# Hosted modulation units spread over whole feed-forward stages, two wide groups in the delta stage, tables in eight pieces

## The reference, cut to what matters

```python
# first block, per layer (6 vectors of 1024)
mod = silu(c) @ ada_w[layer] + ada_b[layer]
# second block, per layer (9 vectors of 1024), for two conditions c and c_ctx
m = silu(cond) @ w_mod[l] + b_mod[l]
# every sublayer
h = rmsnorm(x) * (1 + scale) + shift
x = x + gate * sublayer(h)
# feed-forward, hidden width 2816
y = (silu(h @ w_gate) * (h @ w_up)) @ w_out
```

## Time and profile before

| what | value |
|---|---|
| median of 3 runs | 2902.71 us (2901.74 to 2904.06) |
| profiled execution | 2902.25 us |
| its span, first to last instruction | 2900.4 us |
| mean granted clock of PE | 0.946 |
| busy: PE, DVE, ACT | 2601.0, 1778.0, 1039.6 us |
| DMA | 407.56 MB, 141 GB/s in the mean |

### The profile page before, as it was taken

One profiled execution on the slowest core, in us unless ns is written; L12 is line 12 of the kernel. 1 busy time (PEld: TensorE's weight loads), 2 busy tenths in 40 slices (PEclk: granted clock), 3 DMA queues, 4 the chain that ended last, 5 costly groups with the idle time before them and its releaser, 6 DMA issues.

```text
span 2900.4 us, 37201 instructions
## 1 busy us (share of the span) xinstructions
PE 2601.0 (90%) x15014; PEld 2187.0 (75%) x15014; DVE 1778.0 (61%) x2929; ACT 1039.6 (36%) x1572; POOL 53.3 (2%) x56
## 2 busy tenths in 40 slices
PE   5789999787889889999797889999989999888998
PEld 4748998665789867878585567787868888766998
DVE  3546659643476688888836658787453333665655
ACT  4465445511244432222313432222242222434543
POOL 1000000021000000000000000000000000000000
PEclk8989999898899989999898999999999999899999
DMA  8675855434467646666422026575423332431563
GB/s 273 200 221 150 240 172 158 129 117 152 120 172 205 188 124 175 188 183 171 118 65 68 1 73 195 162 200 142 118 85 95 95 95 84 105 82 42 159 188 114
DMA packets 635648, 407.56 MB, mean 141 GB/s; under 512 B 27639, under 2 KB 596694, under 8 KB 634326
## 3 DMA queue, kind: packets, MB, share of 16 engines
q1 hardware_dynamic: 634800, 404.94, 48.6%
q10 hardware_dynamic: 678, 0.25, 0.0%
HBM read 404.09 MB, written 1.05 MB: 140 GB/s over the span
## 4 chain that ended last, share of the span: by engine, by line
PE 78%; DVE 12%; ACT 5%; DMA 2%; issue 2%; ACTq 0%; SPq 0%; POOL 0%; DVEq 0%
PE ps L1508 66%; DVE ada_acc L1759 3%; DVE tmp L1951 1%; PE ps L1519 1%; DVE h_lo L1943 1%; PE ps L1290 1%; PE ps L539 1%; DVE w_lo L1737 1%; PE ps L1267 1%; ACT w_hi L1628 1%; PE ps L801 1%; PE ps L809 1%; DMA wide_rows<-in_ada_w 1%; PE ps L811 1%; DMA raw<-in_attn_w_in 1%
## 5 line engine op out<-in xcount | busy, mean ns | idle before, releaser
L1508 PE MATMUL ps<-h_hi,w_hi 128*128 128x256 f32 (+1 forms) x3048 | 1021.5, 335 | 69.5 <-DVE h_lo L1943 59.4
L1628 ACT CAST w_hi<-raw 128x1024 fp32r<-128x1024 f32 (+3 forms) x557 | 554.8, 996 | 1387.3 <-PE ps L1508 1349.1
L1508 PE MATMUL ps<-h_hi,w_lo 128*128 128x256 f32 (+1 forms) x3048 | 1008.2, 331 | 0.0
L1508 PE MATMUL ps<-h_lo,w_hi 128*128 128x256 f32 (+1 forms) x3048 | 1007.9, 331 | 0.0
L1737 DVE TENSOR_TENSOR w_lo<-raw,w_hi 128x1024 fp32r<-128x1024 f32 (+3 forms) x557 | 644.9, 1158 | 363.5 <-ACT w_hi L1628 361.4
L1508 PEld LDWEIGHTS ps<-h_hi,w_hi 128*128 128x128 f32 x3048 | 589.5, 193 | 144.1 <-issue 69.5
L1508 PEld LDWEIGHTS ps<-h_lo,w_hi 128*128 128x128 f32 x3048 | 590.7, 194 | 50.5
L1508 PEld LDWEIGHTS ps<-h_hi,w_lo 128*128 128x128 f32 x3048 | 591.7, 194 | 47.6
L1508 PE MATMUL ps<-a_hi,w_hi 128*128 128x256 f32 (+1 forms) x1056 | 357.6, 339 | 0.1
L1508 PE MATMUL ps<-a_hi,w_lo 128*128 128x256 f32 (+1 forms) x1056 | 355.9, 337 | 0.0
L1508 PE MATMUL ps<-a_lo,w_hi 128*128 128x256 f32 (+1 forms) x1056 | 355.7, 337 | 0.0
(11 more groups left out here) (313 smaller groups left out, 1926.8 us busy)
## 6 DMA issues: line engine op xcount, KB each, us to landing
raw<-in_ffn_w_in SPq DMA_DIRECT2D x264, 512.0 KB, 4.6
ada_raw<-in_w_mod SPq DMA_DIRECT2D x128, 512.0 KB, 4.0
raw<-in_ffn_w_out SPq DMA_DIRECT2D x96, 512.0 KB, 4.6
wide_rows<-in_ada_w SPq DMA_DIRECT2D x64, 512.0 KB, 5.0
raw<-in_ffn_w_out SPq DMA_DIRECT2D x48, 384.0 KB, 3.4
raw<-in_gdn_w_in SPq DMA_DIRECT2D x33, 512.0 KB, 4.1
raw<-in_w_in SPq DMA_DIRECT2D x26, 512.0 KB, 3.8
raw<-in_attn_w_in SPq DMA_DIRECT2D x24, 512.0 KB, 7.0
```

The source lines that it names most:

```text
L1508: last = mm(ps[0:m, slot, 0:n], w[:, slot, k * P:k * P + m], v[:, s0 + k, 0:n], start=(k == 0 and w is w_hi and v is hi), stop=(k == lin.k ...
L1628: nc.scalar.copy(w_hi[:, slot, 0:n], raw[:, slot, 0:n]).then_inc(s_hi, 1)
```

## The change

The tiles of `HOSTS` span whole feed-forwards, across stage borders, and units are evenly spread over them: 2 first units in the projection as before; 8 first units over the 68 tiles of the first block's layer 0 feed-forward; none in layer 1's; 12 second units over feed-forward 1 and 10 over feed-forward 2 of the second block's layer 0; 8 over feed-forward 1 of its layer 1. There are two wide groups in the delta stage instead of three: group 2 with G = 0 and group 3 with G = 1, with products after levels 4, 5, 6 and after the first five state steps; turned and written at the end of each G. The tables come as eight DMAs, after tiles 4, 6, ... 18, and the three small DMAs after tile 6; angles are made at step 16, sines at step 20. A hosted pair is loaded at least three tiles after the one that it is used with.

```diff
-WIDES = (("first", 6, "attention", 6), ("first", 10, "attention", 7),
-         ("first", 16, "delta", 7), ("first", 20, "delta", 3), ("second", 0, "delta", 7))
+HOSTS = ((4, 2, ("attn_w_in", 0), ("attn_w_in", 0)), (14, 8, ("ffn_w_in", 0), ("ffn_w_out", 0)),
+         (30, 12, ("ffn1_w_in_2", 0), ("ffn1_w_out_2", 0)), (42, 10, ("ffn2_w_in_2", 0), ("ffn2_w_out_2", 0)),
+         (52, 8, ("ffn1_w_in_2", 1), ("ffn1_w_out_2", 1)))
+WIDES = ((6, "attention", 6), (10, "attention", 7), (22, "delta", 7), (26, "delta", 7))
+SECOND = 2 * 2 * MOD1
...
+def hosted_units(stages):
+    pairs, sums, order = {}, {}, {}
+    for unit0, count, first, last in HOSTS:
+        tiles = [s.g0 + j for s in stages if isinstance(s, Linear) and s.weight in (first, last) for j in range(s.n)]
+        for u in range(count):
+            a, b = (tiles[0] + (len(tiles) - 1) * (u + i) // count for i in range(2))
+            order[unit0 + u] = len(order)
+            for k in range(KD // 2):
+                g = a + k * (b - a) // (KD // 2)
+                pairs.setdefault(g, []).append((unit0 + u, k))
+            sums[g] = unit0 + u
+    return pairs, sums, order
...
@@ delta_tensor
-                    wide_products(pe, 2 + 2 * G, level)
-                wide_products(pe, 2 + 2 * G, 7)
+                    if level >= 4:
+                        wide_products(pe, 2 + G, level - 4)
                 for n, step in enumerate((turn, first_values, new_state, keys_by_state, second_values, outputs, output_sums)):
                     for s in range(2):
                         step(2 * G + s, s)
-                    if step is new_state:
-                        wide_turned(pe, 2 + 2 * G)
-                    if not G:
-                        wide_products(pe, 3, n)
-                if not G:
-                    wide_products(pe, 3, 7)
-                    wide_turned(pe, 3)
+                    if n < 5:
+                        wide_products(pe, 2 + G, 3 + n)
+                wide_turned(pe, 2 + G)
...
@@ SP
-            def load_tables():
-                sp.dma_start(consts[:, head:], dram["constants"][:, head:]).then_inc(s_rest, 16)
-                sp.dma_start(pos_i[:], dram["positions"].to_broadcast([P, T])).then_inc(s_rest, 16)
+            def load_table(n):
+                a, b = (head + (table.shape[1] - head) * (n + i) // 8 for i in range(2))
+                sp.dma_start(consts[:, a:b], dram["constants"][:, a:b]).then_inc(s_rest, 16)
+            def load_small():
+                sp.dma_start(pos_i[:], dram["positions"].to_broadcast([P, T])).then_inc(s_pos, 16)
...
-                if g == 8:
-                    load_tables()
-                for host, u, k in after_tile.get(g, ()):
-                    unit_pair(host, u, k)
+                if 4 <= g < 20 and g % 2 == 0:
+                    load_table(g // 2 - 2)
+                if g == 6:
+                    load_small()
+                for u, k in after_tile.get(g, ()):
+                    unit_pair(u, k)
...
+            in_order = [(g, pair) for g in sorted(pairs_at) for pair in pairs_at[g]]
+            for p, (g, pair) in enumerate(in_order):
+                earliest = in_order[p - 2][0] + 6 if p >= 2 else 0
+                after_tile.setdefault(max(earliest, g + 3), []).append(pair)
```

More of the change, by code:

```diff
@@ L133, with __init__ @@
 class Linear:
-    def __init__(self, kind, weight, kt, n, tokens, row0=0, offsets=None, stride=BODY * P, loads=None, ada=None, **more):
+    def __init__(self, kind, weight, kt, n, tokens, row0=0, offsets=None, stride=BODY * P, loads=None, **more):
         self.kind, self.weight, self.kt, self.n, self.tokens = kind, weight, kt, n, tokens
-        self.row0, self.offsets, self.stride, self.loads, self.ada = row0, offsets, stride, loads, ada
+        self.row0, self.offsets, self.stride, self.loads = row0, offsets, stride, loads
         self.more = more
@@ L151, in pieces @@
         return [(0, j // BODY * self.stride + self.offsets[j % BODY], P)]
[L153 to L168, removed]
     def columns(self, j):
@@ L236, in number @@
 def number(stages):
-    g = h_blocks = a_blocks = units = rows = norms = subs = silus = sqs = ssqs = 0
+    g = h_blocks = a_blocks = norms = subs = silus = sqs = ssqs = 0
     slot_dmas = [0] * RING
@@ L284, in number @@
         elif s[0] == "attention":
-            stages[i] = ("attention", h_blocks, units)
-            units += 4 * sum(w[2] == "attention" for w in WIDES)
+            stages[i] = ("attention", h_blocks)
             h_blocks += KD
         elif s[0] == "delta":
-            stages[i] = ("delta", h_blocks, units)
-            units += 4 * sum(w[2] == "delta" for w in WIDES)
+            stages[i] = ("delta", h_blocks)
             h_blocks += HEADS
@@ L498, in units_before @@
             i = next(n for n, s in enumerate(stages) if s is st)
[L499 to L506, removed]
+            earlier = [s[0] for s in stages[:i] if not isinstance(s, Linear)]
+            return FIRST_UNITS + sum(g < tiles_before(st) for g in sum_at) + 4 * sum(w[1] in earlier for w in WIDES)
         def blk(j, n=1):
             return proj[:, j * T:(j + n) * T]
-        def wide_before(n):
-            return WIDES[n][1] + (2 * 2 * MOD1 if WIDES[n][0] == "second" else 0)
         def wide_load(sp, n, k):
             i = KD * n + k
-            which, unit0, _, _ = WIDES[n]
-            name, per = ("ada_w", 2 * MOD1) if which == "first" else ("w_mod_2", 2 * MOD2)
             if i >= 2:
@@ L1067, in delta_vector @@
                         step(2 * G + s, s)
-                    if step is second_rhs:
-                        wide_columns(dve, 2 + 2 * G)
-                if not G:
-                    wide_columns(dve, 3)
+                wide_columns(dve, 2 + G)
         def delta_gpsimd(pool, st):
@@ L1510, in tile, with unit_sums @@
                 last.then_inc(s_tile, 1)
-            def unit_sums(lin, u):
-                dual = lin.ada[0] == "second"
-                pe.wait_ge(s_ada_use, KD * (lin.row_unit0 + u + 1))
-                pe.wait_ge(s_mod, lin.unit0 + u)
-                for c in range(2 if dual else 1):
+            def unit_sums(unit):
+                pe.wait_ge(s_ada_use, KD * (row_unit[unit] + 1))
+                pe.wait_ge(s_mod, unit)
+                for c in range(1 if unit < SECOND else 2):
                     for q in range(4):
@@ L1763, in ada_rows, with ada_sum @@
                     last.then_inc(s_ada_use, 1)
-            def ada_sum(lin, u):
-                which, first, _ = lin.ada
-                dve.wait_ge(s_ada_T, lin.row_unit0 + u + 1)
-                for c in range(2 if which == "second" else 1):
-                    last = V.tensor_reduce(mod_columns(which, c, first + u), ps[:, ADA_A + c, :].rearrange("p (q n) -> p q n", q=4), AX_X, ALU.add)
+            def ada_sum(unit):
+                dve.wait_ge(s_ada_T, row_unit[unit] + 1)
+                for c in range(1 if unit < SECOND else 2):
+                    dst = mod1[:, 4 * unit:4 * unit + 4] if unit < SECOND else mod2[:, c, 4 * (unit - SECOND):4 * (unit - SECOND) + 4]
+                    last = V.tensor_reduce(dst, ps[:, ADA_A + c, :].rearrange("p (q n) -> p q n", q=4), AX_X, ALU.add)
                 last.then_inc(s_mod, 1)
             def angles():
-                dve.wait_ge(s_rest, 64)
+                dve.wait_ge(s_pos, 16)
+                dve.wait_ge(s_rest, 160)
                 link(dve, V.tensor_copy(ang[:, 2, :], pos_i[:]), "dve")
@@ L1896, in _ @@
                             split(*nxt)
-                        for u in st.sums(j - 1):
-                            ada_sum(st, u)
-                        for u, k in st.pairs(j):
-                            ada_rows(st, u, k)
-                        if st.g0 + j == 10:
+                        if st.g0 + j - 1 in sum_at:
+                            ada_sum(sum_at[st.g0 + j - 1])
+                        for unit, k in pairs_at.get(st.g0 + j, ()):
+                            ada_rows(unit, k)
+                        if st.g0 + j == 16:
                             angles()
```

107 lines of the change are left out of this document (44 added, 63 removed).

## The result

The changed kernel takes 2865.26 us (median of 4 runs, 2864.54 to 2868.94) against 2903.39 us of the kernel before beside it: a ratio of 0.9871, 95% interval 0.9854 to 0.9888. The forecast was 2866.1 us. A second measurement on another occasion gave 2866.47 against 2903.14, ratio 0.9872 (0.9857 to 0.9886). The profiled execution took 2864.54 us with a span of 2862.7.

A forecast was written before the change was run, and what follows sets the result against it. PE was taken as full in feed-forwards, with waits for hosted sums on top. Feed-forwards 22.7, delta stage 9.4 and tables 5.5 us, less 1 for seams, saved 36.6, giving 2866.1 us; 8-in-10 range 2851 to 2885.

The forecast's parts named there:

- The yardsticks: Feed-forwards without hosted units, PE full: 368.3 us at 512 tokens, 190.3 at 256; anything beyond is the hosted units' price.
- part 1: Feed-forwards: evenly spread hosted units remove PE's waits where two pairs meet in one step; saves 22.7 us together.
- The price of a sum: PE's cost per hosted unit's sum: 0.9 us at 512 tokens, 1.7 at 256, 2.5 in a kt 6 stage.
- DMA in layer 0: First block's layer 0 feed-forward: 50.7 MB at 247 GB/s, hidden but only just; 1 us added, range 0 to 10.
- The delta stage: Part 2, fewer wide products in merge levels and five between state steps of each G: saves 9.4 us.
- State steps of G = 0: Delta stage, 35.2 us with nine wide products falls to 28.7 with five; saves 6.5 us, while G = 1 loses 0.7.
- outside DVE's work: Delta stage state steps: the part of five wide products' time that DVE's work does not cover, about 1.4 us.
- The projection: Part 3, tables in pieces: unit 4's last pair lands near 78.5, PE waits 4 to 5 us, not 9.3; saves 5.5.
- Crowding was not the cause: Rival for the feed-forwards: DVE stays late whatever the spacing, 20 us less gain, 2886 us; chance 0.12.
- More than counted: Rival: merge levels give 0.8 us each, state steps find their rows, some 256-token waits go; 2853 us, chance 0.12.
- Pieces cost like small DMAs: Rival for the projection: eight table pieces at 1.5 us each; part 3 loses 6 us, 2878 us; chance 0.04.
- the slower one: Rival: first block layer 0 becomes bound by DMA, under 210 GB/s; at 205 GB/s the kernel takes 2908 us; chance 0.02.

The follow-up runs named there:

- experiment 3: Changed kernel with 17 and 13 evenly spread hosted units in second block layer 0's feed-forwards 1 and 2, none in layer 1: 2878.17 us, ratio 0.9908.
- experiment 1: Changed kernel with PE transposing a hosted unit's sums one tile later: 2845.90 us, ratio 0.9794 of the kernel before.
- experiment 6: Changed kernel with each hosted pair of the first block's layer 0 feed-forward loaded twice, the second time into unread rows: 2873.41 us, ratio 0.9896.
- experiment 2: Changed kernel with wide products after every merge level and one after turn, instead of three in levels and five between state steps: 2854.38 us, ratio 0.9826.
- experiment 4: Changed kernel with the table in one DMA and the three small DMAs behind it, after tile 8: 2871.25 us, ratio 0.9883.
- experiment 5: Changed kernel with the table in sixteen pieces, one after each of tiles 4 to 19: 2865.66 us, ratio 0.9872.

## Why the prediction was right, step by step

**The yardsticks.** Everything in part 1 hung on two feed-forwards without hosted units, 368.3 and 190.3 us. They stayed: the last one takes 190.3 us after too, layer 1's feed-forward 1 is back at 368.3 in experiment 3, where it has no units, and with the hosts gone layer 1 of the first block takes 189.3, 1.0 less than its yardstick. I had held back 0.8 of its 8.3 us; nothing needed it.

**The price of a sum.** 0.9 us for a second unit at 512 tokens, 1.7 for a first one at 256, 2.5 in a kt 6 stage. After, 27 sums at 512 tokens outside kt 6 stages are all followed by the next tile without a wait; the three in kt 6 stages waited 2.35, 1.40 and 1.13 us; those at 256 tokens 1.02 to 1.03 in `swiglu` and 1.19 in `residual` stages, and 2.72 in the kt 6 one, for which I had only 2.5 with the transposes; with them it cost about 3.2. That mis-sized term is more than half of the 1.2 us by which the first block's layer 0 came out worse. The three long feed-forwards are within 0.7 us each. The causes given are shown by experiment 1 (the wait is where the sum stands) and, with the two limits found there, experiment 3 (crowding).

**DMA in layer 0.** Forecast hidden at 247 GB/s plus 1 us; it was 240 GB/s at a share of 0.81, and experiment 6 shows the room above. That the stage from 320.0 to 369.5 had hosted at this density was the right row to go by.

**The delta stage** was 2.4 us too good. Levels 1 to 3 lose 0.43 us each, not 0.45, right; but the first level with a product takes 7.26 us and not 6.60 (experiment 2), which I had not seen, 0.7 us in each G. From the start of the stage, or of G = 1, to level 6's product the two G gained 2.4 us together, forecast 3.6. State steps of G = 0 gained 6.2 of 6.5, and G = 1 lost 1.6 where 0.7 was forecast; these three make up the 2.4. Inside the state steps errors met that nearly cancel. The base after all subtractions was 23.8 us, from a stretch in which PE had its lower clock about a third of the time (that is what a mean of 0.82 between full and half clock comes to), and the steps take 21.8 without any product on their chain (experiment 2): 2.0 too much. The five products were priced at 1.4 us "outside DVE's work", and four of them cost 3.0 by subtraction; the waits for loads were 4.2 and 4.7 us, forecast 3.5. The sum, 28.7 against 29.0 and 29.6, was nearly right, its terms not, and that is luck.

**The projection** gained 7.2 instead of 5.5: the wait was 2.9 us, forecast 4 to 5. The path that I gave for it was wrong. I had it hang on the landing of unit 4's last pair, put at 78.5 us. The pair landed at 76.3, but what ended the wait was weight tile 11, before the change too (experiment 4), and that this tile gained 6.6 us (81.60 to 74.96) where the pair gained 0.7 (77.0 to 76.3) is nothing that I had worked out; after it the pair is a close second, 0.9 us ahead of its use. That the size is near is luck. Nor did the clock stay up: PE's products follow each other 0.21 us apart and not 0.12 for some 3 us behind the wait (80.2 to 83.5), before the change for some 4 (86.2 to 90.6).

**The total** is better than its parts. The stages came out 4.4 us worse than forecast in four places (1.2, 2.4, 0.7 and 0.1) and 3.6 better in three (1.7, 1.8 and 0.1). That it came within 1 us of 2865.26 is partly luck; a single term was good to 1 or 2 us.

**The rivals.** "Crowding was not the cause" is refuted as it stood, but 17 units did need more than spreading. "More than counted" came true in neither of its parts. "Pieces cost like small DMAs" is refuted by experiment 5, the slower one by 6.

**What stays open:** the order of the pairs alone in the projection (2.9 us of its gain are left to it by subtraction, not by a run); and what a product in the state steps would cost with its rows already there, since no run separates the four further products from their loads.

## What to carry to other kernels

Look for a stage of the same shape without the guest work: it gives the price of the guest closely (the three long feed-forwards came out within 0.7 us), and the sum over stages forecasts the whole. A consumer that stands in program order right behind its producer waits at any spacing wherever its own engine comes round sooner than the producer ends (at 256 tokens and in kt 6 stages here, not in the longer tiles of 512 tokens); put it one step later and the wait is gone, which here was worth half as much as the whole change. Fill waits with work where the engine would stand anyway (0.43 us for a product of 1.0 in the merge levels), not in a chain of steps that go by faster than the work's data come: there four products more cost 7.2 us with their loads. And when one engine waits for an operation of another, look in the chain at what that other engine had to do just ahead of it: in the projection it was the split of a late weight tile, not the pair.

## What the hardware showed that I had not expected

- PE's clock makes a poor base out of a stretch with a stop in it: 24.3 us (0.85 of them transposes that stand in the chain there only) at a granted clock of 0.82 on average, against 21.8 us for the same steps in windows with 0.91 and 0.88.
- The 16 DMA engines gave 316 GB/s in the mean of 205 us with weight tiles, of which each piece is 512 bytes wide, and 2 KB rows mixed. The profile's DMA share was 1.09 in that stretch, so a share of 1 is not the limit; 255 GB/s at a share of 0.85 (318.1 to 366 of the changed kernel) is 81% of what was reached.
- A DMA of 139 KB cost no more for its bytes than one of 279 KB, in a queue with others behind it.
